# New x of a feed stays in PSUM: norm weight in y's copy, three fed outputs, unused products, a weight half split by columns

## The chip, the cores and the metric

One core of one Trainium2 chip. The metric is the device time in microseconds of one execution of the kernel. Engines are named as the profile does: PE is TensorE (PEld its weight loads), DVE is VectorE, ACT is ScalarE, POOL is GpSimd, SP the queue that issues all DMAs.

## What is computed

One inference step of a two-layer decoder trunk, for a prompt of 256 positions and eight samples of one position. The residual stream x thus has 264 columns; D is 1024. Each layer adds three branches, every one between two RMS norms:

```
def rms_norm(x, g):
    xf = x.astype(jnp.float32)
    y = xf * lax.rsqrt(jnp.mean(xf * xf, axis=-1, keepdims=True) + NORM_EPS)
    return (y * g.astype(jnp.float32)).astype(x.dtype)
def swiglu(x, w_gate, w_up, w_down):
    return (jax.nn.silu(x @ w_gate) * (x @ w_up)) @ w_down
def ffn_half_step(x, g_pre, g_post, w_gate, w_up, w_down):
    return x + 0.5 * rms_norm(swiglu(rms_norm(x, g_pre), w_gate, w_up, w_down), g_post)
```

The middle branch is `x + rms_norm(W_out mix(W_in rms_norm(x)))`, where mix holds four groups of heads (dilated window attention, forgetting attention, gated DeltaNet, spatial gating), fed by one projection of 3084 columns.

## The kernel before

x lies in SBUF transposed: 8 tiles (KT) of 128 channels by 264 columns (N). Every matrix product is done in two-part precision: `hi` on ScalarE rounds a weight buffer `raw` to `whi`, `lo` on VectorE makes `wlo = raw - whi`; an input is split the same way into `nhi` (ScalarE) and `nlo` (VectorE). `three` on TensorE then adds three products (L1503 to L1505: whi with hi, whi with lo, wlo with hi).

Weights come in pairs, one per stream s = 0, 1, each stream with one `raw`, `whi` and `wlo` buffer of 128 x 2048 (8 k-tiles of 256 columns, so two outputs of 128). A split is done in two halves of 1024 elements, which are the k-tiles 0 to 3 and 4 to 7. SP loads a stream's next pair when both halves of its `wlo` are made. The six groups of a layer, in order: gu1 (11 pairs, gate and up), dn1 (8), wi (7), the mixers, wo (2), gu2 (11), dn2 (8). Each engine's order is written out by hand, with semaphores (`S`, `V`) between the engines.

Branches and norms are numbered e = 0 to 5 in each layer: even ones are norms of x ahead of gu1, wi and gu2, odd ones norms of a branch's output y. A hand-over from y to the next group is called a feed here. Before the change it goes so:

- ScalarE copies each y tile to `yt` and squares it to `sq` (`evac_y`); GpSimd adds the eight squares to `ss_acc` (`sumsq`); TensorE sums over the partitions (`ss`, a product with a constant matrix, into PSUM bank 7); ScalarE makes the norm factor from it by logarithm and exponential (`rms_of`, L633 and L634).
- VectorE, in `post`, does for each of the 8 tiles: product of `yt`, the norm weight and the factor into a PSUM bank (L986), addition to x in SBUF (L987), and the nlo of the tile before (`lo_n`, L1003). ScalarE, in `pre`, makes nhi (L644) and the square of new x (L645) of each tile.
- TensorE, in `first_pair`, takes the tiles as they come for the two outputs of stream 0 (`by_tile`, 6 products a tile), then the two outputs of stream 1 (`wide_chunk`, 24 products each), and between these the sum of squares of x, `ss(e)`, which is ready behind them. The norm of x is applied after the products: r is multiplied into the results.
- The next group's first weights are split around this: both halves of stream 1 (`hi`, `lo`) stand ahead of the norm factor on ScalarE and ahead of `post` on VectorE.

After the last feed (e = 5 of layer 1), TensorE transposes x tile by tile (L1912, L1913) and ScalarE copies it out.

Of the kernel before, what the change touches and what calls it, by code (L numbers as in the profile page):

```python
# [62 lines left out]
def constants():  # L63
# [81 lines left out]
    "x_new": 24, "y_copied": 24, "y_mm0": 6, "y_mm1": 6, "ys0": 6, "ys1": 6, "z_mm0": 6, "z_mm1": 6,  # L145
# [3 lines left out]
def build(nc, io):  # L149
# [14 lines left out]
    with ctx:  # L164
# [162 lines left out]
        def kt_view(ap, k):  # L327
            return ap.rearrange("p (k m) -> p k m", k=k)


        with nc.Block() as blk:
# [250 lines left out]
            def _(act):  # L582
                ch = Chain(act, "act_ch")
                for l in range(DEPTH):
# [12 lines left out]

                    def gu_step(k, j, nxt, first=False):
# [14 lines left out]
                    def evac_y(n, e, t, bank, s, i):  # L613

                        act.activation(yt[:, bass.ds(t, 1), :].rearrange("p o n -> p (o n)"), ps[:, bank, 0:N], ACT.Copy).then_inc(S("y_copied"), 1)  # L615
                        act.activation(sq8[:, bass.ds(t, 1), :].rearrange("p o n -> p (o n)"), ps[:, bank, 0:N], ACT.Square).then_inc(S("sq"), 1)  # L616

                    def dn_pair(k, q, nxt, ahead=0):
                        n, e = f"dn{k}", {1: 1, 2: 5}[k]
                        for m in range(2):  # L620
                            j = 2 * q + m
                            if nxt[m]:
                                hi(*nxt[m], 0, ahead=ahead * m)
                            act.wait_ge(S("mm_done1"), V("mm_done1", M0[n] + j + 1))
                            evac_y(n, e, j, 4 + m, 1, 0)
                            if nxt[m]:
                                hi(*nxt[m], 1, ahead=ahead * m)

                    def rms_of(e):

                        act.wait_ge(S("ss"), V("ss", e + 1))
                        r = ps[:, 6, 0:N] if e % 2 else r_pre
# [7 lines left out]
                    def pre(e, ahead=0):  # L640

                        for t in range(KT):
                            act.wait_ge(S("x_new"), V("x_new", 8 * (e // 2) + t + 1, ahead))
                            act.activation(nhi[:, t, :], x[:, t, :], ACT.Copy, scale=gain(l + ahead, e, t)).then_inc(S("n_hi"), 1)  # L644
                            act.activation(sq8[:, t, :], x[:, t, :], ACT.Square).then_inc(S("sq"), 1)  # L645


                    if l == 0:
# [4 lines left out]
                        hi("gu1", 0, 1)  # L653
# [13 lines left out]
                    rms_of(1)  # L667
# [145 lines left out]
                    for j in range(WO_P):  # L813
                        nxt = ("wo", 1) if j == 0 else ("gu2", 0)
                        for s in range(2):
                            for i in range(2):
                                act.wait_ge(S(f"mm_done{s}"), V(f"mm_done{s}", M0["wo"] + 2 * j + i + 1))
                                evac_y("wo", 3, 4 * j + 2 * s + i, 2 * s + i, s, i)
                            hi(*nxt, s)
                    rms_of(3)  # L820
# [11 lines left out]
                    rms_of(5)  # L832
# [11 lines left out]
            def _(pool):  # L844
# [5 lines left out]
                for l in range(DEPTH):  # L850
# [3 lines left out]
                    def sumsq(e):  # L854
# [3 lines left out]
                        for t in range(2, KT):  # L858
                            pool.wait_ge(S("sq"), V("sq", 8 * e + t + 1))
                            ins = tt_(ss_acc[:, :], ss_acc[:, :], sq8[:, t, :], ALU.add)  # L860
                            if t < KT - 1:
# [83 lines left out]
            def _(dve):  # L945
                ch = Chain(dve, "dve_ch")
                for l in range(DEPTH):
# [8 lines left out]

                    def gu_step(k, j, nxt):
# [22 lines left out]
                    def post(e):  # L980

                        rsqrt_of(e)
                        dve.wait_ge(S("y_copied"), V("y_copied", 8 * (e // 2 + 1)))
                        for t in range(KT):
                            u = ps[:, 4 + t % 2, 0:N]
# [964 lines left out]
```

## Time and profile before

| | |
|---|---|
| median of 3 runs | 1501.36 us (1497.37 to 1503.3) |
| the profiled execution | 1499.49 us |
| its span, first to last instruction | 1497.7 us |
| mean granted TensorE clock | 0.907 |
| TensorE busy | 1301.9 us (87%) |
| VectorE busy | 907.1 us (61%) |
| ScalarE busy | 617.2 us (41%) |
| GpSimd busy | 229.1 us (15%) |
| read from HBM | 228.65 MB |

Busy is the time in which an engine had an instruction of its own running; matmuls overlap, so a busy TensorE is not one at its peak rate. The clock is the share that the chip granted of TensorE's full speed, 2.4 GHz at 1.00 and 1.2 GHz at 0.50. Times in rows are microseconds from the start of the span.

### The profile page before, as it was taken

Reading aid. Unit: us, or ns where it says so; the run is one execution under the profiler, and the core shown is the slowest. Engines: PE = TensorE matmul, PEld = TensorE weight load, DVE = VectorE, ACT = ScalarE, POOL = GpSimd, SP = SyncE. Lnnn points to the kernel's source line nnn. Section 1 sums busy time; section 2 is a strip of 40 time slices with the busy share of each in tenths; the row PEclk is TensorE's granted clock in tenths of the full one; section 3 lists DMA queues with packets and bytes.
Section 4 is the critical chain, followed back from the end, with each engine's and each line's share of the span. In section 5 each row is a group of like instructions: output and inputs, shape, how many; then the busy total and the mean of one; then the engine's idle time right before and its main releaser. Section 6 shows DMA issues by size and latency. Waiting matters only on the chain.

```text
span 1497.7 us, 27870 instructions
## 1 busy us (share of the span) xinstructions
PE 1301.9 (87%) x9864; PEld 1210.7 (81%) x9864; DVE 907.1 (61%) x1524; ACT 617.2 (41%) x1151; POOL 229.1 (15%) x238
## 2 busy tenths in 40 slices
PE   6999997995568789999989999799845888799997
PEld 5999997974456579999979999799624757799996
DVE  3666436567775557664466764654776565666643
ACT  4665344324120255444465644533430204544443
POOL 2000001005274020000010000100163621100000
PEclk9999998985689699999989999899766888999998
DMA  6555563553454235555645655644455524355563
GB/s 227 170 181 176 145 201 123 165 170 95 150 187 149 85 116 166 176 182 154 192 148 170 195 162 157 189 142 138 129 177 152 157 90 140 112 185 181 156 173 93
DMA packets 286119, 234.15 MB, mean 156 GB/s; under 512 B 19898, under 2 KB 282018, under 8 KB 286056
## 3 DMA queue, kind: packets, MB, share of 16 engines
q1 hardware_dynamic: 286056, 233.37, 50.9%
q8 instruction: 32, 0.52, 0.1%
q14 instruction: 31, 0.25, 0.1%
HBM read 228.65 MB, written 5.37 MB: 156 GB/s over the span
## 4 chain that ended last, share of the span: by engine, by line
PE 68%; DVE 16%; issue 6%; ACT 3%; DMA 3%; POOL 2%; SPq 2%; DVEq 0%; POOLq 0%; ACTq 0%
PE ps L1503 19%; PE ps L1504 19%; PE ps L1505 19%; DVE wlo L955 3%; PE ps L1731 2%; PE ps L1839 2%; PE ps L1838 2%; DVE nlo L1003 2%; DVE s L1203 2%; POOL kslot L933 1%; ACT whi L596 1%; DVE ps L986 1%; DMA raw<-in_ffn_down_dram 1%; DMA raw<-in_w_in_dram 1%; PE ps L1822 1%
## 5 line engine op out<-in xcount | busy, mean ns | idle before, releaser
L1503 PE MATMUL ps<-nhi,whi 128*128 128x264 f32 x1936 | 561.5, 290 | 38.4 <-DVE nlo L1003 27.8
L955 DVE TENSOR_TENSOR wlo<-raw,whi 128x1024 fp32r<-128x1024 f32 (+2 forms) x376 | 394.7, 1091 | 273.5 <-ACT whi L596 273.0
L1504 PE MATMUL ps<-nlo,whi 128*128 128x264 f32 x1936 | 556.1, 287 | 0.0
L1505 PE MATMUL ps<-nhi,wlo 128*128 128x264 f32 x1936 | 555.5, 287 | 0.0
L1503 PEld LDWEIGHTS ps<-nhi,whi 128*128 128x128 f32 x1936 | 372.7, 193 | 44.7 <-DVE nlo L1003 20.9
L596 ACT ACTIVATE whi<-raw 128x1024 fp32r<-128x1024 f32 (+2 forms) x376 | 336.8, 945 | 169.4 <-PE ps L1505 112.2
L1504 PEld LDWEIGHTS ps<-nlo,whi 128*128 128x128 f32 x1936 | 372.9, 193 | 0.2
L1505 PEld LDWEIGHTS ps<-nhi,wlo 128*128 128x128 f32 x1936 | 370.7, 191 | 0.0
L1503 PE MATMUL ps<-hhi,whi 128*128 128x264 f32 x704 | 201.7, 287 | 9.4 <-DVE hlo L972 9.1
L1505 PE MATMUL ps<-hhi,wlo 128*128 128x264 f32 x704 | 200.8, 285 | 0.0
L1504 PE MATMUL ps<-hlo,whi 128*128 128x264 f32 x704 | 200.3, 285 | 0.0
L1503 PEld LDWEIGHTS ps<-hhi,whi 128*128 128x128 f32 x704 | 133.2, 189 | 10.6 <-issue 9.8
L1505 PEld LDWEIGHTS ps<-hhi,wlo 128*128 128x128 f32 x704 | 133.4, 189 | 0.0
L1504 PEld LDWEIGHTS ps<-hlo,whi 128*128 128x128 f32 x704 | 133.2, 189 | 0.0
L857 POOL TENSOR_TENSOR ss_acc<-sq 128x264 f32<-128x264 f32 x12 | 9.0, 751 | 726.1 <-ACT sq L616 692.0
L609 ACT ACTIVATE hhi<-h_t 128x264 f32 (+1 forms) x88 | 37.3, 424 | 164.2 <-DVE h_t L969 164.2
L933 POOL TENSOR_TENSOR kslot<-kslot,q_bc 128x512 f32<-128x512 f32 x64 | 87.3, 1392 | 81.1 <-DMA kslot<-in_state_swa_k_dram 42.0
L860 POOL TENSOR_TENSOR ss_acc<-ss_acc,sq 128x264 f32<-128x264 f32 x72 | 57.1, 793 | 222.1 <-ACT sq L616 200.4
L972 DVE TENSOR_TENSOR hlo<-h_t,hhi 128x264 f32 (+1 forms) x88 | 38.2, 434 | 59.9 <-ACT hhi L609 59.9
L604 ACT ACTIVATE s_t<-s_t 128x264 f32<-128x264 f32 x88 | 35.6, 424 | 57.5 <-DVE s_t L962 57.4
L962 DVE TENSOR_TENSOR s_t<-ps,ptr 128x264 f32<-128x264 f32 x88 | 36.0, 427 | 37.7 <-ACT ptr L634 29.3
L615 ACT ACTIVATE yt<-ps 128x264 f32 (+1 forms) x48 | 18.8, 391 | 90.8 <-PE ps L1505 90.6
(343 smaller groups left out, 1409.1 us busy)
## 6 DMA issues: line engine op xcount, KB each, us to landing
raw<-in_ffn_gate_dram SPq DMA_DIRECT2D x44, 1024.0 KB, 5.3
raw<-in_ffn_up_dram SPq DMA_DIRECT2D x44, 1024.0 KB, 5.3
raw<-in_ffn_down_dram SPq DMA_DIRECT2D x64, 704.0 KB, 4.6
raw<-in_w_in_dram SPq DMA_DIRECT2D x24, 1024.0 KB, 5.8
kslot<-in_cache_fox_k_dram SPq DMA_DIRECT2D x128, 128.0 KB, 2.8
vslot<-in_cache_fox_v_dram SPq DMA_DIRECT2D x128, 128.0 KB, 2.6
raw<-in_w_out_dram SPq DMA_DIRECT2D x8, 1024.0 KB, 5.1
kslot<-in_state_swa_k_dram SPq DMA_DIRECT2D x32, 128.0 KB, 2.7
```

The lines of the kernel that those rows point to most:

```text
L596: act.activation(whi[s][:, a:b], raw[s][:, a:b], ACT.Copy).then_inc(S(f"w_hi{s}"), 1)
L604: act.activation(s_t[:, f, :], s_t[:, f, :], ACT.Silu).then_inc(S("silu"), 1)
L609: act.activation(hhi[:, bass.ds(2 * j + f, 1), :].rearrange("p o n -> p (o n)"), h_t[:, f, :], ACT.Copy).then_inc(S("h_hi"), 1)
L860: ins = tt_(ss_acc[:, :], ss_acc[:, :], sq8[:, t, :], ALU.add)
L933: ins = tt_(kslot[:, i, g:g + 2, :], kslot[:, i, g:g + 2, :], q_bc[:, i, GW:512].unsqueeze(1).broadcast_to([P, 2, GW]), ALU.mult)
L955: tt2(wlo[s][:, a:b], raw[s][:, a:b], whi[s][:, a:b].bitcast(F32), ALU.subtract).then_inc(S(f"w_lo{s}"), 1)
L962: tt2(s_t[:, f, :], ps[:, f, 0:N], r_pre, ALU.mult).then_inc(S("gate_taken"), 1)
L972: tt2(hlo[:, at, :].rearrange("p o n -> p (o n)"), h_t[:, f, :], hhi[:, at, :].rearrange("p o n -> p (o n)").bitcast(F32), ALU.subtract).t ...
L1003: stt(nlo[:, t, :], x[:, t, :], gain(l + ahead, e, t), nhi[:, t, :].bitcast(F32), ALU.mult, ALU.subtract).then_inc(S("n_ready"), 1)
L1503: mm(out, wh, hi_, start=first, stop=False)
L1504: mm(out, wh, lo_, start=False, stop=False)
L1505: return mm(out, wl, hi_, start=False, stop=last)
```

## The change

- *New x stays in PSUM* for a feed. VectorE writes product and sum into one of three PSUM banks (`x_bank`: 4, 6, 5 in turn). nhi and nlo are made from there, and ScalarE copies x back to SBUF (`x_kept`), a third instruction a tile; it squares the SBUF copy one tile later. VectorE's nlo waits for that copy too. At the very end x goes to SBUF directly (`to_x`).
- *The product of `post` runs one tile ahead* (`scaled(t + 1)` before the addition of t). The norm weight is multiplied in by ScalarE's copy of y (`copy_y` has a scale), so the product is tensor by tensor.
- *The last y tile*: it is squared first and copied only after the norm factor (`branch_end`); GpSimd adds seven squares only, TensorE adds the eighth by a second product with the constant matrix.
- *Three fed outputs*: `first_pair` takes three outputs with the tiles (9 products a tile), then the sum of squares, then the fourth output (24 products). It starts with one tile ready, not two.
- *Unused matmuls*: `keep_busy` puts 24 products of weights with weights ahead of five feeds, into a bank that the next real product overwrites.
- *Split by columns*: stream 1's first weights are split in two halves by output (`hi_first`, `lo_first`; 8 x 128 elements each), the first ahead of the factor and of `post`, the second behind them.

```diff
+        def x_bank(t):
+            return ps[:, (4, 6, 5)[t % 3], 0:N]
+        def columns(w, i):
+            return kt_view(w[:, :], KT)[:, :, i * P:(i + 1) * P]
...
+                    def hi_first(n, i, ahead=0):
+                        act.wait_ge(S("w_raw1"), V("w_raw1", 16 * (P0[n] + 1), ahead))
+                        if M0[n] or l + ahead:
+                            act.wait_ge(S("mm_done1"), V("mm_done1", M0[n], ahead))
+                        act.activation(columns(whi[1], i), columns(raw[1], i), ACT.Copy).then_inc(S("w_hi1"), 1)
...
+                    def branch_end(e, bank, nxt, ahead=0):
+                        if nxt:
+                            hi_first(nxt[0], 0, ahead)
+                        rms_of(e)
+                        copy_y(e, KT - 1, bank)
+                        if nxt:
+                            hi_first(nxt[0], 1, ahead)
...
                         for t in range(KT):
-                            act.wait_ge(S("x_new"), V("x_new", 8 * (e // 2) + t + 1, ahead))
-                            act.activation(nhi[:, t, :], x[:, t, :], ACT.Copy, scale=gain(l + ahead, e, t)).then_inc(S("n_hi"), 1)
-                            act.activation(sq8[:, t, :], x[:, t, :], ACT.Square).then_inc(S("sq"), 1)
+                            act.wait_ge(S("x_new"), V("x_new", b + t + 1, ahead))
+                            src = x[:, t, :] if at_start else x_bank(t)
+                            act.activation(nhi[:, t, :], src, ACT.Copy, scale=gain(l + ahead, e, t)).then_inc(S("n_hi"), 1)
+                            if not at_start:
+                                act.activation(x[:, t, :], src, ACT.Copy).then_inc(S("x_kept"), 1)
+                            if t:
+                                square_x(t - 1)
+                        square_x(KT - 1)
...
+                        def scaled(t):
+                            if t in (0, 2):
+                                dve.wait_ge(S("y_copied"), V("y_copied", b + (KT if t else KT - 1)))
+                            if t >= 3 and to_x:
+                                dve.wait_ge(S("x_new"), V("x_new", b + 8 + t - 2))
+                            elif t >= 3:
+                                dve.wait_ge(S("x_kept"), V("x_kept", b + t - 2))
+                                dve.wait_ge(S("n_ready"), V("n_ready", b + 8 + t - 2))
+                            tt2(x_bank(t), yt[:, t, :], ps[:, 7, 0:N], ALU.mult).then_inc(S("scaled"), 1)
...
                         for t in range(KT):
-                            u = ps[:, 4 + t % 2, 0:N]
-                            ch(stt(u, yt[:, t, :], gain(l, e, t), ps[:, 6, 0:N], ALU.mult, ALU.mult))
-                            tt2(x[:, t, :], x[:, t, :], u, ALU.add).then_inc(S("x_new"), 1)
+                            if t + 1 < KT:
+                                scaled(t + 1)
+                            dve.wait_ge(S("scaled"), V("scaled", b + t + 1))
+                            tt2(x[:, t, :] if to_x else x_bank(t), x[:, t, :], x_bank(t), ALU.add).then_inc(S("x_new"), 1)
...
+                    def keep_busy(n):
+                        for part in range(2):
+                            split_ready(n, 0, 0, part)
+                        for _ in range(24):
+                            mm(ps[:, 0, 0:N], whi[0][:, 0:P], whi[0][:, P:P + N], start=True, stop=True)
                     def first_pair(n, e):
-                        by_tile(n, "n_ready", 8 * (e // 2))
-                        wide_chunk(n, 0, 1, (2, 3), lambda i: ss(e) if i else None)
+                        for k in range(KT):
+                            pe.wait_ge(S("n_ready"), V("n_ready", 8 * (e // 2) + max(k + 1, 3 if e == 0 and l == 0 else 1)))
+                            for s, i in ((0, 0), (0, 1), (1, 0)):
...
+                        ss(e)
+                        split_ready(n, 0, 1, 1)
+                        for k in range(KT):
+                            ins = three(ps[:, 3, 0:N], 1, k * 256 + P, nhi[:, k, :], nlo[:, k, :], k == 0, k == KT - 1)
...
-                        mm(ps[:, 7, 0:N], C("mean"), ss_acc[:, :], start=True, stop=True).then_inc(S("ss"), 1)
+                        ins = mm(ps[:, 7, 0:N], C("mean"), ss_acc[:, :], start=True, stop=e % 2 == 0)
+                        if e % 2:
+                            pe.wait_ge(S("sq"), V("sq", 8 * (e + 1)))
+                            ins = mm(ps[:, 7, 0:N], C("mean"), sq8[:, KT - 1, :], start=False, stop=True)
```

VectorE at the feed from wo to gu2 in layer 0, before the change (the wlo rows are the last weight splits ahead of it; L986 is the product, L987 the addition, L1003 nlo of the tile before):

```order
L955 TENSOR_TENSOR wlo_76<-raw_72,whi_74 128x1024 x2
L955 TENSOR_TENSOR wlo_77<-raw_73,whi_75 128x1024 x2
L986 SCALAR_TENSOR_TENSOR ps<-yt,gains,ps 128x264
L987 TENSOR_TENSOR x<-x,ps 128x264
L986 SCALAR_TENSOR_TENSOR ps<-yt,gains,ps 128x264
L987 TENSOR_TENSOR x<-x,ps 128x264
L1003 SCALAR_TENSOR_TENSOR nlo<-x,gains,nhi 128x264
```

And in the changed kernel (L1011 is `lo_first`, L1051 the product, L1060 the addition, L1080 nlo):

```order
L1006 TENSOR_TENSOR wlo_76<-raw_72,whi_74 128x1024 x2
L1011 TENSOR_TENSOR wlo_77<-raw_73,whi_75 128x8x128
L1051 TENSOR_TENSOR ps<-yt,ps 128x264 x2
L1060 TENSOR_TENSOR ps<-x,ps 128x264
L1051 TENSOR_TENSOR ps<-yt,ps 128x264
L1060 TENSOR_TENSOR ps<-x,ps 128x264
L1080 SCALAR_TENSOR_TENSOR nlo<-ps,gains,nhi 128x264
```

One half of stream 1's lo has left its place ahead of the feed, the product is one tile ahead, and x is written to PSUM.

ScalarE at the same feed, before (the last y tile's copy and square, the split of stream 1, the norm factor, then new x):

```order
L615 ACTIVATE yt<-ps 128x264
L616 ACTIVATE sq_94<-ps 128x264
L596 ACTIVATE whi_75<-raw_73 128x1024 x2
L633 ACTIVATE ps<-ps,const 128x264
L634 ACTIVATE ps<-ps 128x264
L644 ACTIVATE nhi<-x,gains 128x264
L645 ACTIVATE sq_94<-x 128x264
```

And now (L611 is `hi_first`, L631 the copy of y, L635 the squares of the last two y tiles):

```order
L635 ACTIVATE sq_94<-ps 128x264 x2
L611 ACTIVATE whi_75<-raw_73 128x8x128
L667 ACTIVATE ps<-ps,const 128x264
L668 ACTIVATE ps<-ps 128x264
L631 ACTIVATE yt<-ps,gains 128x264
L611 ACTIVATE whi_75<-raw_73 128x8x128
L688 ACTIVATE nhi<-ps,gains 128x264
L690 ACTIVATE x<-ps 128x264
L688 ACTIVATE nhi<-ps,gains 128x264
L690 ACTIVATE x<-ps 128x264
L683 ACTIVATE sq_94<-x 128x264
```

The last copy of y and one half split have moved behind the norm factor, and each tile of new x has a third instruction, L690.

TensorE there, before, from the sum of squares of y to the first products on new x:

```order
L1555 MATMUL ps<-ss_acc,const 128x264
L1503 MATMUL ps<-nhi,whi_74 128x264
L1504 MATMUL ps<-nlo,whi_74 128x264
L1505 MATMUL ps<-nhi,wlo_76 128x264
L1503 MATMUL ps<-nhi,whi_74 128x264
```

And now:

```order
L1658 MATMUL ps<-ss_acc,const 128x264
L1661 MATMUL ps<-sq_94,const 128x264
L1618 MATMUL ps<-whi_74 128x264 x24
L1585 MATMUL ps<-nhi,whi_74 128x264
L1586 MATMUL ps<-nlo,whi_74 128x264
L1587 MATMUL ps<-nhi,wlo_76 128x264
L1585 MATMUL ps<-nhi,whi_74 128x264
L1586 MATMUL ps<-nlo,whi_74 128x264
L1587 MATMUL ps<-nhi,wlo_76 128x264
L1585 MATMUL ps<-nhi,whi_75 128x264
```

A second sum product and 24 unused ones stand ahead of the feed, and the third output of each tile is of stream 1 (whi_75).

## Rows read from the trace of the kernel before

**Rows 1.** The page, part 4: shares of the chain of waits by engine.

```profile
PE 68%; DVE 16%; issue 6%; ACT 3%; DMA 3%; POOL 2%; SPq 2%; DVEq 0%; POOLq 0%; ACTq 0%
```

**Rows 2.** Stretches: length, busy of PE PEld DVE ACT POOL, clock, DMA share, GB/s.

```profile
223.53:232.73 9.20, 1.25 (x4) 0.54 (x3) 8.56 (x13) 6.71 (x13) 2.09 (x2) 0.64 0.65 211
541.65:549.46 7.81, 0.71 (x3) 0.30 (x3) 6.03 (x11) 5.66 (x12) 1.48 (x2) 0.85 0.69 224
748.81:756.62 7.81, 0.72 (x3) 0.30 (x3) 6.03 (x11) 5.64 (x12) 2.26 (x3) 0.69 0.39 119
...
sum 41.40, PE 4.65 PEld 1.97 DVE 34.75 ACT 29.95 POOL 9.40; mean PE 0.93 PEld 0.39 DVE 6.95 ACT 5.99 POOL 1.88
...
549.46:553.80 4.34, 4.34 (x19) 4.34 (x20) 4.24 (x10) 2.34 (x7) 2.24 (x3) 0.50 0.21 70
557.00:564.00 7.00, 7.00 (x59) 6.93 (x58) 1.27 (x4) 2.20 (x4) 0.75 (x1) 1.00 0.00 0
```

**Rows 3.** Timeline of PE, wo to gu2, layer 0: start, length, what, [idle <-releaser].

```profile
543.29 0.71 PE L1555 MATMUL ps<-ss_acc,const 128*128 128x264 f32 x2 [1.65 <-POOL ss_acc L860]
549.46 0.59 PE L1503 MATMUL ps<-nhi,whi 128*128 128x264 f32 x1 [5.45 <-DVE nlo L1003]
...
561.12 0.39 PE L1555 MATMUL ps<-ss_acc,const 128*128 128x264 f32 x1
...
571.57 0.36 PE L1503 MATMUL ps<-nhi,whi 128*128 128x264 f32 x1 [0.53 <-DVE wlo L955]
```

**Rows 4.** Timeline of ACT at the same feed.

```profile
541.68 0.39 ACT L615 ACTIVATE yt<-ps 128x264 f32<-128x264 f32 x1 [2.23 <-PE ps L1505]
...
542.24 2.00 ACT L596 ACTIVATE whi<-raw 128x1024 fp32r<-128x1024 f32 x2
544.13 0.46 ACT L633 ACTIVATE ps<-ps,const 128x264 f32<-128x264 f32 x1
544.62 0.38 ACT L634 ACTIVATE ps<-ps 128x264 f32<-128x264 f32 x1
546.60 0.51 ACT L644 ACTIVATE nhi<-x,gains 128x264 fp32r<-128x264 f32 x1 [1.60 <-DVE x L987]
```

**Rows 5.** Timeline of DVE at the same feed.

```profile
543.33 2.36 DVE L955 TENSOR_TENSOR wlo<-raw,whi 128x1024 fp32r<-128x1024 f32 x2 [3.43 <-ACT whi L596]
545.61 0.49 DVE L986 SCALAR_TENSOR_TENSOR ps<-yt,gains,ps 128x264 f32<-128x264 f32 x1
546.13 0.43 DVE L987 TENSOR_TENSOR x<-x,ps 128x264 f32<-128x264 f32 x1
...
547.35 0.49 DVE L1003 SCALAR_TENSOR_TENSOR nlo<-x,gains,nhi 128x264 fp32r<-128x264 f32 x1
...
548.63 0.78 DVE L1003 SCALAR_TENSOR_TENSOR nlo<-x,gains,nhi 128x264 fp32r<-128x264 f32 x1
...
556.70 0.49 DVE L1003 SCALAR_TENSOR_TENSOR nlo<-x,gains,nhi 128x264 fp32r<-128x264 f32 x1
```

**Rows 6.** Timelines of ACT and DVE, pair 1 of that gu2.

```profile
562.61 1.04 ACT L596 ACTIVATE whi<-raw 128x1024 fp32r<-128x1024 f32 x1
...
570.20 1.23 DVE L955 TENSOR_TENSOR wlo<-raw,whi 128x1024 fp32r<-128x1024 f32 x1 [0.38 <-ACT whi L596]
```

**Rows 7.** Timeline of ACT at dn1 to wi, layer 0.

```profile
225.26 2.00 ACT L596 ACTIVATE whi<-raw 128x1024 fp32r<-128x1024 f32 x2 [0.33 <-DMA raw<-in_w_in_dram]
```

**Rows 8.** All instructions of line 987: duration ns min/median/max, first and last start.

```profile
L987 DVE TENSOR_TENSOR x<-x,ps x48: 428/428/431, 229.2 to 1492.3; 128x264 f32<-128x264 f32 x48
```

**Rows 9.** The page, part 6 (median us to landing), then SP's timeline in layer 1.

```profile
raw<-in_ffn_up_dram SPq DMA_DIRECT2D x44, 1024.0 KB, 5.3
...
raw<-in_w_in_dram SPq DMA_DIRECT2D x24, 1024.0 KB, 5.8
...
762.86 0.42 SPq L349 DMA_DIRECT2D raw<-in_ffn_gate_dram  x1
```

**Rows 10.** Timeline of DVE at the start of layer 0.

```profile
18.01 2.42 DVE L955 TENSOR_TENSOR wlo<-raw,whi 128x1024 fp32r<-128x1024 f32 x2 [0.40 <-ACT whi L596]
```

More of the change, by code:

```diff
@@ L652, in _ @@
                         hi("gu1", 0, 0)
-                        hi("gu1", 0, 1)
+                        for i in range(2):
+                            hi_first("gu1", i)
                         act.wait_ge(S("const_in"), 48)
@@ L857, in sumsq @@
                         ch(tt_(ss_acc[:, :], sq8[:, 0, :], sq8[:, 1, :], ALU.add))
-                        for t in range(2, KT):
+                        tiles = KT - e % 2
+                        for t in range(2, tiles):
                             pool.wait_ge(S("sq"), V("sq", 8 * e + t + 1))
                             ins = tt_(ss_acc[:, :], ss_acc[:, :], sq8[:, t, :], ALU.add)
-                            if t < KT - 1:
+                            if t < tiles - 1:
                                 ch(ins)
@@ L1002, in lo_n @@
                         dve.wait_ge(S("x_new"), V("x_new", 8 * (e // 2) + t + 1, ahead))
-                        stt(nlo[:, t, :], x[:, t, :], gain(l + ahead, e, t), nhi[:, t, :].bitcast(F32), ALU.mult, ALU.subtract).then_inc(S("n_ready"), 1)
+                        at_start = e == 0 and l + ahead == 0
+                        src = x[:, t, :] if at_start else x_bank(t)
+                        if not at_start:
+                            dve.wait_ge(S("x_kept"), V("x_kept", 8 * (e // 2) + t + 1, ahead) - 8)
+                        stt(nlo[:, t, :], src, gain(l + ahead, e, t), nhi[:, t, :].bitcast(F32), ALU.mult, ALU.subtract).then_inc(S("n_ready"), 1)
                     def take_gains(of):
@@ L1027, in _ @@
                         lo("gu1", 0, 0)
-                        lo("gu1", 0, 1)
+                        for i in range(2):
+                            lo_first("gu1", i)
                         dve.wait_ge(S("const_in"), 48)
@@ L1475, in _ @@
                         lo("wo", 1, s)
-                    for s in range(2):
-                        lo("gu2", 0, s)
+                    lo("gu2", 0, 0)
+                    lo_first("gu2", 0)
                     post(3)
+                    lo_first("gu2", 1)
                     rsqrt_of(4)
@@ L1488, in _ @@
                     if l + 1 < DEPTH:
-                        for s in range(2):
-                            lo("gu1", 0, s, ahead=1)
+                        lo("gu1", 0, 0, ahead=1)
+                        lo_first("gu1", 0, ahead=1)
                     post(5)
+                    if l + 1 < DEPTH:
+                        lo_first("gu1", 1, ahead=1)
             @blk.tensor
@@ L1573, in _ @@
                         pe.wait_ge(S("const_in"), 48)
+                    else:
+                        keep_busy("gu1")
                     first_pair("gu1", 0)
@@ L1896, in _ @@
                     ss(3)
+                    keep_busy("gu2")
                     first_pair("gu2", 4)
```

61 lines of the change are left out of this document (47 added, 14 removed).

## Prediction

> **What bounds the kernel now.** I read the page's chain of waits first [rows 1]: 68% of the span is TensorE, nearly all of it the three lines of the split products. So time goes where TensorE is idle or paced by others. Next the timeline of TensorE for its idle stretches outside the mixers, then the table of stretches. At five places the residual stream is handed from one weight group to the next (dn1 to wi and wo to gu2 in both layers, dn2 to gu1 between them). From the last product of y to the first product on new x, 41.4 us pass in these five, and TensorE works 4.65 us of them [rows 2]. That is the field of this change; a sixth hand-over is the end of the kernel.
>
> I take wo to gu2 of layer 0 as the pattern. The last y product ends 1.65 us before 543.29, at 541.64 [rows 3]. ScalarE copies it (541.68, 0.39), squares it, splits the second weight buffer in two halves (542.24 to 544.24), and only then reaches the logarithm (544.13, started as the half drains) and the exponential, which ends at 545.00 [rows 4]. GpSimd's addition ends at 543.29 and TensorE's sum at 544.00 [rows 3], so ScalarE's own order is about as late as the sum. VectorE makes the second lo half until 545.69 and starts on y at 545.61 [rows 5]: the norm factor and VectorE's weight halves tie, the halves a little later. Then come eight tiles, and the last nlo runs from 556.70 to 557.19 [rows 5], 1.45 us a tile. TensorE begins at 549.46 after 5.45 us idle; it waits for two tiles. After the last tile it has 6 products of that tile and 48 of the second buffer, and the sum of squares of x stands behind 24 of these, at 561.12 [rows 3]. From this norm factor hangs a serial chain: Exp, split of pair 1 (562.61), silu, h, split, lo (570.20) [rows 6], and TensorE starts pair 1's second buffer at 571.57 after 0.53 idle [rows 3].
>
> **The change, part by part,** for that feed.
>
> *1. The start.* The last square goes ahead of the copy, GpSimd's last addition goes (TensorE adds the eighth square itself), and one half of the split, not two, stands before the logarithm. The square, as long as the copy, ends near 542.06, and TensorE's sum takes 0.71 [rows 3]: 542.85. ScalarE's half split, 1.06, starts as the square drains and ends near 543.0; logarithm 0.46 and Exp 0.38 follow, to 543.9 instead of 545.00. VectorE makes one lo half (1.2, half of 2.36 [rows 5]) from 543.05 and starts on y at 544.17: **1.44 earlier**. In the w_in feeds the raw weights are late (the split starts at 225.26, released by a DMA [rows 7]): half split to 226.3, lo half to 227.5, then y. There the waiting stretch is 9.20 long instead of 7.81 [rows 2] because two halves follow that landing; one half less of 1.15 is what is gained.
>
> *2. The tiles.* Now a tile is product 0.49 with a hand-over (0.52 from start to start), addition 0.35 from start to start, lo 0.41, or 0.78 long where GpSimd adds beside it [rows 5]. After it is product 0.35 (tensor by tensor, one tile ahead, so no hand-over), addition 0.35, lo 0.49, and 0.03 until its end is seen, since the next bank is written only then: 1.22. The 0.43 of both tensor-by-tensor forms rests on L987, which has a PSUM input today: 428 to 431 ns in all 48, GpSimd beside it or not [rows 8]. A lo with x in PSUM has no row; the ends are 0.49 and 0.78, the two kinds of L1003 [rows 5]; I take 0.49, since L986 and L987, which read PSUM, keep their time beside GpSimd. ScalarE has three instructions a tile: 0.51, the copy back and a square about 0.39 each, as L615 [rows 4]; with the 0.1 by which they overlap each that is 1.0 to 1.1, and its copy of a tile ends some 0.3 before VectorE needs it. The first nlo ends 2.65 after the start, the last 10.4 after it (11.6 now): **1.2 earlier**. If the cover fails, the pitch stays near 1.45: 8 x 0.23 = 1.8 us a feed.
>
> *3. TensorE in the tiles.* Nine products a tile instead of six: 9 x 0.119 = 1.07 at clock 1.00 (59 in 7.00 us), under the 1.22 of a tile; at clock 0.50 they would take 9 x 0.228 = 2.05 (19 in 4.34) [rows 2]. After the last tile 9 + 24 products remain instead of 6 + 48: 21 x 0.119 = **2.5 less**. The sum of squares stands ahead of all 24 of the rest, so the chain behind the norm factor starts 2.5 earlier too. GpSimd's last addition ends near 11.7 after the start, TensorE's tile 7 near 11.6; a tie.
>
> *4. The unused products.* 24 x 0.119 = 2.9 us, from 542.9 to 545.8 at full clock, while the first tile is ready near 546.8: they cost nothing and leave 1 us idle. Today the clock is at 0.50 while TensorE works from 549.46 to 553.80 [rows 2], yet it caught up before the last tile, so keeping the clock wins nothing by itself; it makes part 3 possible. The Trainium skill (TensorE: Matmul & The Clock Gate, What's actually happening) says that the throttled state is the default and activity releases it; the trace agrees as far as it goes, with 0.64, 0.85 and 0.69 granted in three of these waits.
>
> *5. The rest of a pair.* The first pair ends 1.44 + 1.2 + 2.5 = 5.2 earlier. Pair 1's first buffer may wait 0.8 for its lo; its second buffer starts by the chain, 9.0 behind the split at 562.61, and that moves by the same 5.2: 571.57 becomes **566.4**. The load of the second buffer for pair 1 now waits for the lo half behind the feed: issued near 555.9, landing 5.3 later [rows 9] at 561.2. It is wanted one half split, 1.04, before the lo at 570.20 less 5.2 [rows 6]: 563.9, cover 2.7 us. Behind it on SP's queue stand only loads of pair 2, which wait for later releases anyway. In w_in landing takes 5.8 [rows 9]: there at 244.9, wanted near 246.4.
>
> Per feed: gu2 twice 5.2; wi twice 1.15 + 1.2 + 2.5, some 5.0 with its hand-overs. gu1 of layer 1 less: SP issues pair 1's raw only at 762.86, behind the loads of parameters, so it lands near 768.2 [rows 9], and the split that starts near 769.8 now (562.61 + 207.16, the distance of the two feeds [rows 2]) can move by 1.5 only, or by 2.9 if SP gets on sooner, since GpSimd's memset loses the addition ahead of it; I take 2.7. The start of layer 0 loses: its order now wants the third half of lo, 18.01 + 3 x 1.2 = 21.6 [rows 10], where it began near 19.4, with 6 products (1.3 us at half clock) in between: 0.5 us. The end gains 1.0 at its start, and 7 x 0.17 = 1.2 if additions 0.70 apart instead of 0.87 set its pace, or nothing if its transposes do; I take 1.4 together.
>
> Sum: 2 x 5.2 + 2 x 5.0 + 2.7 - 0.5 + 1.4 = **24.0 us**. The profiled execution took 1499.49 (span 1497.7): 1475.5 after. The median of the runs shown stands 1.9 higher, 1477.4 by that. I say 1476.5.
>
> **Rivals.**
>
> *The tile pitch stays* (ScalarE's three instructions pace it, or lo takes 0.78). For it: only 0.3 us of cover. Against: rows 8. 5 x 1.8 = 9 less: gain 15, 1486. Chance 0.09.
>
> *A PSUM input makes VectorE dearer.* Three instructions a tile have one now, against one or two before. If each grew by 0.06, the step from 0.43 to 0.49 that the rows show between two forms, a tile takes 0.18 more: 8 x 0.18 x 5 = 7 less, 1483.5. Against: L987 reads PSUM and is the shortest. The Trainium skill (VectorE: DVE Perf Modes, The TRN2 errata) gives VectorE 58 cycles of fixed cost from SBUF and 120 from PSUM, which would be 65 ns each and 1.6 us a feed, an estimate from the skill's figures; the trace does not bear it out. Chance 0.05.
>
> *The clock falls all the same.* For it: TensorE still has gaps near 1 us on both sides of the unused products. Then these take 5.5 and end at 548.4, 1.6 after the first tile, and tiles run at 2.05 until near 553, the rest at 1.07, done near 559.1 instead of 555.8: 3.3 less a feed. In all five: gain 7.5, 1492. Against: TensorE's share of work there goes from a tenth to over six tenths. Chance 0.09.
>
> *Slower.* The second stream's load, now behind the feed, becomes the bound. It decides once landing takes 5.3 + 2.7 + 5.2 = 13.2 us instead of 5.3 in every feed, with the saving gone: at 15 us each loses 1.8, 1509. DMA engines at 0.69 busy in these stretches [rows 2] speak for some room only. Chance 0.04.
>
> *No effect* (the mixers wait for cache pages and give it back, or hand-offs eat it): 1499. Chance 0.04.
>
> **Numbers.** Forecast 0.69, with its own range 1471 to 1482: a fifth of the sum either way, and runs that spread by 6 us. The range for 8 in 10 takes in the rivals on pitch: 1470 to 1488. Under 0.5% (7.5 us) a measurement of this kernel can hardly tell from no change; the clock rival lies on that border and counts by two thirds as faster. Faster 0.89, same 0.06, slower 0.05.
>
> **What will show it.** VectorE starts on y 2.5 us after the last y product (4.0 now); additions start 1.22 apart (1.4 speaks for the pitch rival); granted clock 1.00 through the feed, product starts 0.12 apart (0.22: clock rival); 33 products after the last nlo; pair 1's second buffer 24.8 us after the last y product (29.9 now). No DMA ends a wait in pair 1, except in gu1 of layer 1. Wrong if ScalarE ends VectorE's waits in every tile, or raw ends them in wi.

## The result, and the profile after it

| | before | after |
|---|---|---|
| median, same chip (4 runs each) | 1499.78 us (1497.37 to 1503.3) | 1485.37 us (1484.38 to 1486.34) |
| profiled execution, its span | 1499.49, 1497.7 us | 1484.38, 1482.5 us |
| granted clock | 0.907 | 0.92 |
| TensorE, VectorE, ScalarE, GpSimd busy | 1301.9, 907.1, 617.2, 229.1 us | 1318.4, 901.7, 629.4, 227.8 us |

The ratio is 0.9888 (95% interval 0.9862 to 0.9914). 1476.5 was forecast, 1470 to 1488 as the range: the time lies in the range and 8.9 us above the number. The saving was 14.4 us by the medians and 15.1 by the two spans, against a sum of 24.0.

The chain of waits by engine, the page's part 4, after [rows 1]:

```profile
PE 70%; DVE 14%; issue 6%; ACT 3%; POOL 3%; SPq 2%; DMA 2%; DVEq 0%; ACTq 0%; POOLq 0%
```

The five stretches from the end of the last product of y to the first product on new x, columns as in [rows 2]:

```profile
224.05:230.73 6.68, 4.29 (x28) 3.28 (x27) 5.73 (x9) 5.68 (x12) 0.00 (x0) 1.00 0.53 166
541.06:546.19 5.13, 4.04 (x29) 3.35 (x27) 3.42 (x7) 4.83 (x11) 0.00 (x0) 1.00 0.56 191
...
sum 28.55, PE 20.70 PEld 16.62 DVE 21.44 ACT 25.64 POOL 0.83; mean PE 4.14 PEld 3.32 DVE 4.29 ACT 5.13 POOL 0.17
```

These waiting stretches shrank from 41.40 to 28.55 us, and the clock in them is 1.00. TensorE at the feed from wo to gu2 of layer 0, with the rows that answer to [rows 3]:

```profile
540.53 0.29 PE L1585 MATMUL ps<-nhi,whi 128*128 128x264 f32 x1
...
541.54 0.71 PE L1661 MATMUL ps<-sq,const 128*128 128x264 f32 x2
541.90 3.24 PE L1618 MATMUL ps<-whi 128*128 128x264 f32 x24
546.19 0.39 PE L1585 MATMUL ps<-nhi,whi 128*128 128x264 f32 x1 [1.06 <-DVE nlo L1080]
...
556.83 0.71 PE L1658 MATMUL ps<-ss_acc,const 128*128 128x264 f32 x2 [0.69 <-POOL ss_acc L911]
...
567.37 0.36 PE L1585 MATMUL ps<-nhi,whi 128*128 128x264 f32 x1 [0.51 <-DVE wlo L1006]
```

The L1618 row is the 24 unused products. New is the idle time before 556.83: TensorE has done every tile and waits 0.69 us for GpSimd. VectorE there (L1051 is the product, L1060 the addition, L1080 nlo, L1011 the half of lo behind the feed; compare [rows 5]):

```profile
542.47 1.22 DVE L1011 TENSOR_TENSOR wlo<-raw,whi 128x1024 fp32r<-128x1024 f32 x1 [3.06 <-ACT whi L611]
543.61 0.77 DVE L1051 TENSOR_TENSOR ps<-yt,ps 128x264 f32<-128x264 f32 x2
...
548.80 0.44 DVE L1051 TENSOR_TENSOR ps<-yt,ps 128x264 f32<-128x264 f32 x1
549.14 0.43 DVE L1060 TENSOR_TENSOR ps<-x,ps 128x264 f32<-128x264 f32 x1
549.48 0.48 DVE L1080 SCALAR_TENSOR_TENSOR nlo<-ps,gains,nhi 128x264 fp32r<-128x264 f32 x1
550.07 0.44 DVE L1051 TENSOR_TENSOR ps<-yt,ps 128x264 f32<-128x264 f32 x1
...
554.01 0.49 DVE L1080 SCALAR_TENSOR_TENSOR nlo<-ps,gains,nhi 128x264 fp32r<-128x264 f32 x1 [0.47 <-ACT x L690]
554.42 1.75 DVE L1011 TENSOR_TENSOR wlo<-raw,whi 128x1024 fp32r<-128x1024 f32 x1
```

GpSimd's last two additions, in one row:

```profile
554.34 2.44 POOL L911 TENSOR_TENSOR ss_acc<-ss_acc,sq 128x264 f32<-128x264 f32 x2 [0.20 <-ACT sq L683]
```

All 66 additions of L911 have a median of 757 ns and a maximum of 1606. The longest ones are the last of a feed: of the two in this row, the first (0.76) has begun when VectorE's half lo starts, and the second, which starts while the half lo runs and ends 0.60 behind it, takes 1.60. So 0.85 of the 2.44 us is extra. The half lo itself, 1.22 ahead of the feed, takes 1.75. Both instructions read only SBUF. The instructions with a PSUM operand, all of L1060 and L1080, columns as in [rows 8]:

```profile
L1060 DVE TENSOR_TENSOR ps<-x,ps x40: 426/430/432, 228.8 to 1276.0; 128x264 f32<-128x264 f32 x40
...
L1080 DVE SCALAR_TENSOR_TENSOR nlo<-ps,gains,nhi x40: 483/487/494, 230.2 to 1277.6; 128x264 fp32r<-128x264 f32 x40
L1080 DVE SCALAR_TENSOR_TENSOR nlo<-x,gains,nhi x8: 483/625/862, 10.4 to 16.0; 128x264 fp32r<-128x264 f32 x8
```

From the traces I worked out where the span went. A feed runs from the start of the last group of three products of y (540.53) to pair 1's second buffer (567.37); A and D lead to wi, B and E to gu2, C to gu1 of layer 1. "dn" are the four stretches from the last group of gu to the last of dn, the mixers those from the last of wi to the last of wo. "Start" is the time up to pair 1's second buffer in gu1 of layer 0, "end" the time from the last group of dn2 of layer 1 on.

| us | start | A | B | C | D | E | dn, sum | mixers | end |
|---|---|---|---|---|---|---|---|---|---|
| before | 44.65 | 30.98 | 30.46 | 30.44 | 30.52 | 30.47 | 269.79 | 232.39, 232.01 | 15.84 |
| after | 45.06 | 27.75 | 26.84 | 27.19 | 27.37 | 26.84 | 272.28 | 234.53, 231.16 | 13.43 |

The feeds gave 16.9, the end 2.4; the start took 0.4, the dn stretches 2.5 and the mixers 1.3. The rest, 550.1 us, is the same in both. That makes 15.1.

The dn stretches hold no changed code. In each of them TensorE waits 2.07 to 2.41 us for the last hlo and then works either at full or at half clock. The first 3.24 us behind that wait in dn2 of layer 0, after:

```profile
680.07:683.31 3.24, 3.24 (x14) 3.24 (x15) 1.91 (x5) 0.56 (x1) 0.00 (x0) 0.50 0.10 26
```

The same kernel in another execution (e11 below):

```profile
679.45:682.69 3.24, 3.24 (x26) 3.24 (x27) 1.91 (x5) 0.57 (x1) 0.00 (x0) 1.00 0.07 19
```

14 products against 26, with the same code and the same wait of 2.07 us ahead. A fall in dn2 costs 1.45 us: dn2 of layer 0 took 66.80 us before and 68.25 after. Before had one such fall in its four stretches, after three.

In the mixer of layer 0 the same 52 products (L1731 and L1733, now L1841 and L1843) took 5.79 us at a granted clock of 0.81 before and 8.57 at 0.53 after. First before and then after:

```profile
408.32:414.11 5.79, 5.79 (x54) 1.77 (x53) 1.39 (x2) 0.00 (x0) 0.00 (x0) 0.81 0.72 235
```

```profile
405.55:414.12 8.57, 8.57 (x54) 2.09 (x53) 1.39 (x2) 0.00 (x0) 0.17 (x1) 0.53 0.81 239
```

### The profile page after: what moved, and what is told of

Same layout as the page of the kernel before. It is cut to its first block, busy times and chain, and to the rows that moved or that the text cites. A ratio compares the mean times of both kernels' runs of the same rounds, so it can differ in the third digit from the quotient of the medians.

```text
span 1482.5 us, 28206 instructions
## 1 busy us (share of the span) xinstructions
PE 1318.4 (89%) x9996; PEld 1221.7 (82%) x9996; DVE 901.7 (61%) x1524; ACT 629.4 (42%) x1191; POOL 227.8 (15%) x232
## 4 chain that ended last, share of the span: by engine, by line
PE 70%; DVE 14%; issue 6%; ACT 3%; POOL 3%; SPq 2%; DMA 2%; DVEq 0%; ACTq 0%; POOLq 0%
PE ps L1585 19%; PE ps L1586 19%; PE ps L1587 19%; PE ps L1841 2%; DVE wlo L1006 2%; PE ps L1949 2%; PE ps L1948 2%; DVE s L1282 2%; POOL kslot L984 1%; DMA raw<-in_w_in_dram 1%; DVE ps L1051 1%; PE ps L1932 1%; ACT whi L604 1%; DVE s L1284 1%; PE ps L1995 1%
## 5 line engine op out<-in xcount | busy, mean ns | idle before, releaser
L1006 DVE TENSOR_TENSOR wlo<-raw,whi 128x1024 fp32r<-128x1024 f32 (+2 forms) x364 | 381.4, 1089 | 267.3 <-ACT whi L604 266.8
L604 ACT ACTIVATE whi<-raw 128x1024 fp32r<-128x1024 f32 (+2 forms) x364 | 324.9, 941 | 166.7 <-PE ps L1587 112.3
L1585 PEld LDWEIGHTS ps<-nhi,whi 128*128 128x128 f32 x1936 | 367.8, 190 | 23.5 <-DVE nlo L1080 6.5
L1586 PEld LDWEIGHTS ps<-nlo,whi 128*128 128x128 f32 x1936 | 368.0, 190 | 0.2
L1587 PEld LDWEIGHTS ps<-nhi,wlo 128*128 128x128 f32 x1936 | 366.1, 189 | 0.0
L911 POOL TENSOR_TENSOR ss_acc<-ss_acc,sq 128x264 f32<-128x264 f32 x66 | 55.9, 847 | 178.1 <-ACT sq L635 165.4
L1028 DVE TENSOR_TENSOR hlo<-h_t,hhi 128x264 f32 (+1 forms) x88 | 38.1, 433 | 59.9 <-ACT hhi L624 59.9
L631 ACT ACTIVATE yt<-ps,gains 128x264 f32 (+1 forms) x48 | 23.1, 481 | 79.5 <-PE ps L1587 79.5
```

Of the source, the lines that this page charges most:

```text
L604: act.activation(whi[s][:, a:b], raw[s][:, a:b], ACT.Copy).then_inc(S(f"w_hi{s}"), 1)
L1006: tt2(wlo[s][:, a:b], raw[s][:, a:b], whi[s][:, a:b].bitcast(F32), ALU.subtract).then_inc(S(f"w_lo{s}"), 1)
L1028: tt2(hlo[:, at, :].rearrange("p o n -> p (o n)"), h_t[:, f, :], hhi[:, at, :].rearrange("p o n -> p (o n)").bitcast(F32), ALU.subtract).t ...
L1585: mm(out, wh, hi_, start=first, stop=False)
L1586: mm(out, wh, lo_, start=False, stop=False)
L1587: return mm(out, wl, hi_, start=False, stop=last)
```

## The experiments

All edits are on the changed kernel. The measure beside each is before on the same chip: 1498.43, 1500.4, 1500.35 and 1500.8 us in the four sets.

**e1, no unused products.**

```diff
-                        keep_busy("gu1")
-                    keep_busy("wi")
-                    keep_busy("gu2")
```

> The changed kernel without the 24 unused products ahead of the five feeds; nothing else differs. Theory A (the unused products hold the clock, and with nine products a tile TensorE needs it): the granted clock falls to 0.50 inside the feeds, the 72 products of the tiles end about 2 us later in each (some 12 instead of 10 us long), and the kernel is 6 to 12 us slower than the changed one, near 1494. Theory B (TensorE has slack in the tiles, the unused products are idle ballast): tiles end with the last nlo either way, 1484 to 1487.

1489.85 us (1486.92 to 1497.22), ratio 0.9934 (0.9911 to 0.9956). Only A and C grew, to 29.00 and 28.63; B, D and E stayed at 26.84, 27.31 and 26.86, although the clock fell in them too. In B:

```profile
550.00:553.00 3.00, 3.00 (x15) 3.00 (x15) 2.79 (x8) 2.51 (x7) 1.17 (x2) 0.50 0.02 5
```

Products start 0.22 us apart here, so nine take 2.0 us, more than a tile of 1.28, and TensorE falls behind. GpSimd's late sum gives it the time to catch up: of the 0.69 us that TensorE waits for it in after, 0.07 are left in B. The clock is at 0.50 from 6.0 to 9.4 us after the start of B and from 3.5 to 13.7 after that of A; there the delay shows. In C the sum of squares starts only 0.52 later. The rest of its 1.44 is no clock: the load of pair 1 landed 1.4 later than in after, and C ends with that load (see e10).

**e2, two outputs with the tiles.** The order of TensorE from before: two outputs with the tiles, 24 products, the sum of squares, 24 products.

```diff
-                            for s, i in ((0, 0), (0, 1), (1, 0)):
+                            for s, i in ((0, 0), (0, 1)):
...
+                        for k in range(KT):
+                            ins = three(ps[:, 2, 0:N], 1, k * 256, nhi[:, k, :], nlo[:, k, :], k == 0, k == KT - 1)
```

> The changed kernel with the old order of the first pair: two outputs take the tiles (6 products a tile), the third follows with 24 products, then the sum of squares of x, then the fourth. Theory A (the sum of squares starts the serial chain of the next pair): it starts 1.7 us later in each of the five feeds (48 + 6 products end 4.1 us after the last nlo against GpSimd's addition at 2.3), 8 to 9 us slower than the changed kernel, near 1494. Theory B (the chain has slack, TensorE's order is free): within 2 us of the changed kernel.

1491.41 us (1489.19 to 1496.09), ratio 0.9941 (0.9917 to 0.9964). The feeds sum to 143.08 against 135.99. B takes 28.21, 1.37 more, and its sum of squares starts 17.77 after the last y instead of 16.30. So the third output gives 1.4 a feed and not 2.5: once the products are out of the way, GpSimd's sum comes last.

**e3, seven squares for x.** GpSimd adds seven squares of x as well, TensorE the eighth.

```diff
-                        for t in range(KT - e % 2):
+                        for t in range(KT - 1):
```

> The changed kernel, but for the norms of x too GpSimd adds seven squares only and TensorE adds the eighth by a second product. Theory A (in each feed the sum of squares waits 0.69 us for GpSimd's last addition, which takes 1.60 instead of 0.75 beside VectorE's half lo): the wait goes, the added product takes 0.25 to 0.3, each feed gains 0.35 to 0.45, about 2 us in all, and VectorE's half lo behind the feed takes 1.22 to 1.4 instead of 1.75. Theory B (the tiles' products end as late, 1.6 us after the last nlo, and the added product eats it): no gain, within 1 us.

1486.17 us (1484.24 to 1490.05), ratio 0.9906 (0.9876 to 0.9936). B falls to 26.31. GpSimd is done 1.7 us earlier, but TensorE has a product more, and in D GpSimd's last addition, now the seventh, still takes 1.75 beside the half lo. By the median it is a draw.

**e4, unused products ahead of dn.** 14 of them into bank 7, ahead of the wait for the last h.

```diff
+                        for _ in range(14):
+                            mm(ps[:, 7, 0:N], whi[0][:, 0:P], whi[0][:, P:P + N], start=True, stop=True)
```

> The changed kernel with 14 unused products (1.7 us) also ahead of each of the four down projections, where TensorE waits 2.07 to 2.41 us for the last hlo. Theory A (in the changed kernel this wait costs 1.4 us more at three of the four places, since the granted clock falls to 0.50 behind it): granted clock 1.00 there, 3 to 4.5 us faster, near 1481, unless the mixers' clock moves. Theory B (the 1.45 us lost at dn2 in both layers against the kernel before is not the clock): no gain, 1485.

1481.34 us (1480.99 to 1484.48), ratio 0.9871 (0.9828 to 0.9914). No fall behind the wait in any dn stretch; their sum is 268.93, 3.3 less. The same 3.24 us:

```profile
681.03:684.27 3.24, 3.24 (x28) 3.24 (x28) 1.68 (x5) 0.34 (x1) 0.00 (x0) 1.00 0.15 30
```

**e5, nlo from SBUF.** nlo reads the x that ScalarE copied back.

```diff
-                        src = x[:, t, :] if at_start else x_bank(t)
+                        src = x[:, t, :]
```

> The changed kernel, but VectorE makes nlo from the SBUF copy of x instead of from PSUM. A feed is measured from the start of the last y product to the start of the first product of pair 1's second buffer (26.8 to 27.8 us in the changed kernel, 30.4 to 31.0 before). Theory A (an nlo with three SBUF operands is slowed by GpSimd's addition to 0.78 as before, one from PSUM is not): nlo takes 0.6 to 0.78 in most tiles, tiles 1.4 to 1.5 apart instead of 1.27, feeds longer by 1 to 2 us, 5 to 10 us in all. Theory B (PSUM has no part in it): feeds within 0.2 us of the changed kernel's.

1493.03 us (1490.35 to 1496.99), ratio 0.9951 (0.9925 to 0.9977). Nothing but the place of an input differs. VectorE in B:

```profile
548.44 0.49 DVE L1080 SCALAR_TENSOR_TENSOR nlo<-x,gains,nhi 128x264 fp32r<-128x264 f32 x1
...
549.72 1.04 DVE L1080 SCALAR_TENSOR_TENSOR nlo<-x,gains,nhi 128x264 fp32r<-128x264 f32 x1
```

Of the eight in B, two start beside a running addition of GpSimd and take 1.04, and two more take 0.55. B takes 28.07, 1.2 more; the five together 5.9 more. This is what the PSUM input of nlo is worth: about half of what the change wins in the tiles and behind them.

**e6, both halves of the split ahead.**

```diff
                             hi_first(nxt[0], 0, ahead)
+                            hi_first(nxt[0], 1, ahead)
                         rms_of(e)
```

and both halves of lo ahead of `post`.

> The changed kernel, but both halves of the second buffer's split stand ahead of the norm factor on ScalarE and both lo halves ahead of y's products on VectorE, as before the change (still cut by columns). Theory A (moving one half behind the feed wins 1.2 us at the start and costs 0.7 of it again, since there VectorE's half lo runs beside GpSimd's last addition): VectorE starts 1.15 to 1.2 later, GpSimd's last addition takes 0.75 instead of 1.60, and a feed is 0.5 to 0.6 us longer, 2.5 to 3 us in all. Theory B (nothing is given back behind the feed): a feed is 1.2 us longer, 6 us in all.

1486.18 us (1484.96 to 1487.39), ratio 0.9917 (0.9901 to 0.9934). VectorE starts on y 4.22 us after the start of the last three products instead of 3.08, but GpSimd's last addition takes 0.75 again, so the sum of squares starts only 0.28 later and B takes 27.13. The halved split gives 1.14 at the front and takes back 0.85 behind the tiles. The five feeds sum to 138.49, 2.5 more than in after; the medians differ by 0.8 only.

**e7, the half lo waits for the sum.**

```diff
                     post(1)
+                    dve.wait_ge(S("ss_acc"), V("ss_acc", 3))
                     lo_first("wi", 1)
```

and so in gu2 and gu1.

> The changed kernel, but VectorE's half lo behind the feed waits until GpSimd has made its last addition. Theory A (the two slow each other: 1.60 instead of 0.75 and 1.75 instead of 1.22): GpSimd's last addition takes 0.75 to 0.8, TensorE's sum of squares follows the tiles without the 0.69 of idle time, each feed is 0.5 to 0.7 us shorter, 2.5 to 3.5 us in all; the half lo ends near where it did. Theory B (the sum of squares waits for something else): GpSimd's last addition stays at 1.6 and feeds stay within 0.1 us.

1485.43 us (1483.91 to 1487.65), ratio 0.9909 (0.9892 to 0.9927). Both instructions are back at 0.75 and 1.23 us, and B and E take 26.00, 0.84 less each. C grew to 28.00. There pair 1's load ends the wait (below). The median did not move: the five feeds together took 1.9 less, and dn, with a fall in all four stretches, took as much more (274.23).

**e8, the product right ahead of its own addition.**

```diff
-                        scaled(0)
                         for t in range(KT):
-                            if t + 1 < KT:
-                                scaled(t + 1)
+                            scaled(t)
```

> The changed kernel with each product of y right ahead of its own addition instead of one tile ahead. Theory A (the hand-over from product to addition on VectorE costs 0.1 a tile when it is not covered): tiles 1.35 to 1.4 apart instead of 1.27, feeds 0.6 to 1.0 us longer, 3 to 5 us in all. Theory B (ScalarE's three instructions set the pitch of the tiles): pitch and feeds within 0.1 us of the changed kernel's.

1488.5 us (1486.47 to 1488.96), ratio 0.9931 (0.9915 to 0.9948). Undoing this part shortens B and E to 26.55, 0.29 less. With three banks, the product of t + 1 writes the bank that nlo of t - 2 has just read, and starts 0.10 after that nlo's end (549.96 to 550.07 in the rows of after). In the other order the addition waits 0.46 from the start of its own product instead of 0.35, and the next product does not wait for nlo: 1.21 a tile instead of 1.28. The rest of this kernel's time does not follow: its C took 28.56, its dn stretches 273.8.

**e9, e10, e11: the edits together.** e9 joins e7, e8 and e4; e10 only e7 and e8; e11 is the changed kernel again on the same chip.

> Three single edits put together on the changed kernel: the lo half behind the feed waits for the sum of squares, the product of a tile stands right ahead of its own addition, and 14 unused products into bank 7 stand ahead of each dn group. Theory (the feed is set by VectorE's tile pitch and by GpSimd's last addition, the dn groups by TensorE's clock behind their wait): the feeds B and E take 26.84 less 0.84 less 0.29, 25.7 us each, all five some 130.5 instead of 136.0; the four dn stretches 267 to 269 instead of 272.3; in all about 1476.5 us. Rival (edits are not additive, what one gains the clock or the mixers take back elsewhere): feeds as forecast, but dn stretches and mixers of other runs, 1481 to 1484. Second rival (the two feed edits shorten the same wait): feeds at 26.0, 1479.

> The two feed edits alone (lo half behind the feed waits for the sum of squares; product right ahead of its own addition), no unused products ahead of dn. Theory: feeds B and E 25.7 us, as in the combined kernel; the dn stretches fall to half clock for a while in two or three of the four and sum to 271 to 274; total 1480 us, some 3.5 to 4.5 above the combined kernel. Rival (the unused products ahead of dn do nothing lasting): equal to the combined kernel within 1 us.

> The changed kernel itself again, on the same chip as the two before, as the measure for them. Theory: 1485.4 us as before, ratio 0.989; the combined kernel is 8 to 9 us faster. Rival: this chip gives it 1481 to 1483, and most of what single edits seemed to win (1481.3 for the unused products ahead of dn) is scatter from chip to chip.

| | median | range | ratio to before | feeds A to E | dn |
|---|---|---|---|---|---|
| e9 | 1481.1 | 1480.49 to 1485.8 | 0.9878 (0.9855 to 0.9901) | 26.90, 25.72, 27.43, 26.83, 25.73 | 268.32 |
| e10 | 1485.09 | 1484.11 to 1487.26 | 0.99 (0.9881 to 0.9919) | 26.50, 25.70, 27.79, 26.92, 25.72 | 272.68 |
| e11 | 1485.34 | 1481.82 to 1490.29 | 0.9906 (0.9884 to 0.9928) | 27.73, 26.83, 27.44, 27.36, 26.84 | 269.09 |

B and E came out at the 25.7 that was expected: the two feed edits add up to a hundredth or two. The feed edits by themselves win nothing in the median (e10 against e11), though the two profiles show 3.6 us less in the feeds. In these two profiles dn took 3.6 us more in e10 (clock falls behind three of the four waits, one in e11), which is the same amount; whether that is so in the other executions no trace says. e9 is 4.2 us below e11 by the medians and 4.0 below e10; the intervals of the ratios overlap, so that e9 is faster than the changed kernel is likely and not shown. It has no fall in dn again, and its total is 4.6 us above the 1476.5 expected of it, since C stayed long and the mixers took 2.1 more than in after. It beats e10 only by what the unused products ahead of dn give, and these are 4.4 us of dn between the two profiles. In e10 GpSimd's last two additions take 1.58 together instead of 2.44, and the half lo starts behind them:

```profile
556.02 1.23 DVE L1011 TENSOR_TENSOR wlo<-raw,whi 128x1024 fp32r<-128x1024 f32 x1 [1.44 <-POOL ss_acc L911]
```

```profile
554.41 1.58 POOL L911 TENSOR_TENSOR ss_acc<-ss_acc,sq 128x264 f32<-128x264 f32 x2 [0.46 <-ACT sq L683]
```

Why C does not follow, ScalarE in C of e10:

```profile
763.63 2.00 ACT L604 ACTIVATE whi<-raw 128x1024 fp32r<-128x1024 f32 x2 [1.68 <-DMA raw<-in_ffn_gate_dram]
```

Pair 1's split waits 1.68 us for its weights. Their load stands on SP's queue behind the loads of the next mixer's parameters. Counted from the start of the last three products of y, it was issued at 13.1 in after, 13.7 in e7, 14.1 in e8 and 13.2 in e10, and landed at 18.2, 19.0, 19.6 and 18.8. Pair 1's second buffer starts 9.0 after the landing in all four, and so it does in e1 to e4, e9, e11 and e12. So C of the changed kernel is as long as this load is late, already in after, and the feed edits do not shorten it.

**e12, e10 without the unused products.** The edit of e1.

> The kernel with the two feed edits (lo half behind the feed waits for the sum of squares; product right ahead of its own addition), and without the 24 unused products ahead of the five feeds. In the first run without them only the feeds A and C grew, by 1.25 and 1.44 us; B, D and E kept 26.84, 27.31 and 26.86 although the clock fell in them. Theory (there the late sum of squares, 1.2 us behind TensorE, hid the half clock; with GpSimd on time nothing hides it): now B, D and E lose as well, 0.5 to 1.3 us each against 25.70, 26.92 and 25.72, and all five feeds sum to 136 to 139 us instead of 132.6; in all some 1489 us. Rival (TensorE catches up before the last tile whatever the rest does): B and E stay at 25.7, only A and C grow, sum 135.3, 1488.

1492.49 us (1491.31 to 1493.24), ratio 0.994 (0.9919 to 0.9961), 7.4 above e10, which ran on another chip. Now B and E lose 0.64, D 1.70, A 1.67 and C 0.33; the five sum to 137.60. B and E bear the theory out: the clock is at 0.50 in the same part of the feed as in e1 (6.0 to 9.4 us after its start), where they lost 0.00 and 0.02. The late sum of squares had hidden the half clock. It cannot have hidden more than the 0.69 us that TensorE waits for it in after, so D's 1.70 has a second cause: its clock rose 13.4 us after the start of the feed, against 10.5 in e1. C's 0.33 is its load, which landed 0.34 later. The unused products, worth nothing to B and E while GpSimd's sum comes last, are worth 0.64 each once that wait is gone.

## Why the prediction was right, and what was mis-sized

The direction and the field were right: the gain is in the five feeds, and the change works as said in each. The sum was not. The forecast's own range, 1471 to 1482, was missed by 3.4 us; the time lies in the wider one, which had been drawn to take in the rivals on the tile pitch. So the number was met by the width of the range as much as by the sum.

*The start of y* held: VectorE starts on y 3.08 us after the start of the last three products in B instead of 4.49, 1.41 less (1.44 forecast); in A and D 1.00 and 0.97 less (1.15 forecast). So did 1.00 as the clock in the feeds, [rows 8] for PSUM inputs (430 ns with a PSUM result as well), and nlo at 0.49 in all 40.

*The tiles* gave 0.69, from the start on y to the end of the last nlo (11.59 to 10.90), and 1.2 was forecast. A tile takes 1.28, not 1.22: the product starts 0.10 after the nlo ahead of it and not 0.03. And the last two nlo wait 0.19 and 0.47 for ScalarE's copy back, which was to lie 0.3 ahead.

*TensorE behind the tiles* is the step that failed most. Forecast: 2.5 less, GpSimd's last addition in a tie with TensorE's tile 7. Measured: from the last nlo to the sum of squares 3.93 before, 2.32 after, so 1.6 less; 36 products remain after the last nlo, not 33. GpSimd's last addition ends 13.2 after the start on y and not 11.7: 0.6 of that stays without the overlap (12.3 in e7), 0.85 is the half lo, which the change itself puts beside it and which doubles it. e7 takes the overlap away: there the sum of squares starts 1.47 after the last nlo, 2.46 less than before, which is the 2.5 of the forecast. What failed is thus the tie: the sum had GpSimd's last addition at its usual 0.75.

Per feed that is 1.4 + 0.7 + 1.6 = 3.7, measured 3.6 in B and E against 5.2. In A and D 3.2 against 5.0. C gained 3.25 against 2.7, for SP did get on sooner: it issued the load 14.6 us after the start of the last three products of y before (762.86 [rows 9] less 748.29) and 13.1 after it now (758.63 less 745.53). Together 16.9 instead of 23.1: 6.2 of the 8.9 that the spans missed.

*The start* lost 0.4 (0.5 forecast). *The end* won 2.4, not 1.4: the transposes start 1.0 earlier and also come 0.68 apart instead of 0.87, which is 1.3 over the seven steps; I had counted 0.4 of that. In e11, the same program, the end took 12.86, 0.6 less again, and the start 45.38. *What was costed at nothing*, dn and the mixers, lost 3.8. That part is TensorE's granted clock, two more falls in dn and one longer one in a mixer, in code that did not change. e11 had one fall in dn, at dn1 of layer 0 as before, and the span 1480.0: the same program, 2.5 us less. So the number of falls in dn differs from execution to execution. That the change has no part in it is not shown: before has one trace, with one fall, and the eleven profiles on the changed kernel without unused products ahead of dn have one to four. For the mixer only the traces speak: its stretch took 231 to 237 us in the fourteen profiles, and what sets it was not tried.

*The rivals.* That the tile pitch stays: no, but a third of that rival's price was real (0.5 a feed of 1.8). Dearer PSUM inputs: no. The clock that falls all the same: not in the feeds; e1 shows that by itself it would have cost 1.25 in A, 0.5 in C up to the sum of squares, and nothing in the others. The load as the bound: not in B, D or E, only in C, as [rows 9] said. In A the split of pair 1 does wait for its load (1.73 us; 1.20 in D), which the prediction ruled out for wi and named as a sign of being wrong: the load landed at 246.7 and not at 244.9, for the half lo ahead of its issue ends at 240.7. Yet TensorE's second buffer starts 5.92 after the first, and its 48 products need 5.8: nothing is lost by it.

## What to carry to other kernels

When work is moved off one engine's path, look at what the moved piece will run beside: here a half split put behind the feed doubled GpSimd's addition, which had just become the last arrival, and a sixth of the forecast gain of a feed went there. A filling of unused products is worth what the wait behind them does not already hide, so measure it again when another wait is removed. And a difference of 2 to 4 us in unchanged code is read from the granted clock there before it is put down to the change.

## What the runs showed of the hardware

- VectorE and GpSimd slow each other when both read only SBUF: a GpSimd addition goes from 0.75 to 1.60, VectorE's subtraction of 128x1024 beside it from 1.22 to 1.75, nlo from 0.49 to 0.78 and up to 1.04. It is mainly the one that starts second that grows: in B of e3 the half lo starts beside a running addition and takes 1.75, and that addition keeps its 0.75; in D of e3 the half lo starts first and keeps 1.21, and the addition takes 1.75. With one input from PSUM nlo kept 0.483 to 0.494 in 40 of 40, 30 of which ran beside an addition for some of their time, and these additions kept 0.75 to 0.76.
- TensorE's clock fell to half, or did not, behind the same wait of 2.07 us of the same code in two executions of one kernel; a fall cost 1.45 us. With 14 unused products in the wait it did not fall in any of the eight dn stretches of e4 and e9.
- The Trainium skill (VectorE: DVE Perf Modes, The TRN2 errata) gives PSUM a higher fixed cost than SBUF on VectorE. No run here shows it: the addition takes 430 ns with one PSUM input and a PSUM result, and 418 with one PSUM input and an SBUF result; L1028, from SBUF to SBUF with the same operation, takes 433 in the mean.
